# Eight feed-forward blocks, each with its own SBUF addresses for the split activations

## The reference

```python
def swiglu_ffn(h, w_in, w_out):            # h: [256, 1024], w_in: [1024, 5632], w_out: [2816, 1024]
    gate, up = jnp.split(h @ w_in, 2, axis=-1)
    return (jax.nn.silu(gate) * up) @ w_out

x = x + 0.5 * swiglu_ffn(rms_norm(x, gain), w_in, w_out)
```

## Time and profile before

| | value |
|---|---|
| median of two runs | 2578.5 us (2577.43 to 2579.57) |
| profiled execution, its own time | 2573.3 us |
| its span in the profile | 2571.5 us |
| TensorE busy, matmuls | 2499.3 us, 97% of the span, 23347 matmuls |
| VectorE busy | 1745.9 us, 68% |
| ScalarE busy | 1317.2 us, 51% |
| GpSimd busy | 79.1 us, 3% |
| read from HBM | 421.51 MB, 164 GB/s over the span |
| share of the chain that ended last: TensorE | 85% |

### The profile page before, as it was taken

The page is one execution under the profiler, slowest core; times in us unless marked ns, Lnnn a source line. Parts: engine busy times, 40 slices in busy tenths (PEclk is TensorE's granted clock), DMA queues, the critical chain, the costliest instruction groups (busy, mean ns, idle before and its releaser), DMA issues.

```text
span 2571.5 us, 60615 instructions
## 1 busy us (share of the span) xinstructions
PE 2499.3 (97%) x23347; PEld 2432.0 (95%) x23347; DVE 1745.9 (68%) x2868; ACT 1317.2 (51%) x1997; POOL 79.1 (3%) x122
## 2 busy tenths in 40 slices
PE   8998999999999999999999999899999999999999
PEld 8997877989999999989999999899999999999999
DVE  6757686667757667766756757967666566666774
ACT  5534544455545455555545547465455455555552
POOL 0000452000000000000000000000000000000000
PEclk9999999999999999999999999999999999999999
DMA  5663201535655664545654655245655565553564
GB/s 202 217 216 117 100 11 44 169 127 180 213 176 191 210 214 157 164 140 186 211 165 159 213 167 197 67 132 196 208 169 194 196 179 154 163 157 107 193 210 137
DMA packets 119825, 424.89 MB, mean 165 GB/s; under 512 B 16673, under 2 KB 24564, under 8 KB 119412
## 3 DMA queue, kind: packets, MB, share of 16 engines
q1 hardware_dynamic: 111616, 411.65, 48.4%
q10 hardware_dynamic: 8052, 11.04, 2.3%
HBM read 421.51 MB, written 1.12 MB: 164 GB/s over the span
## 4 chain that ended last, share of the span: by engine, by line
PE 85%; DVE 5%; ACT 2%; issue 2%; POOL 1%; DMA 0%; ACTq 0%; DVEq 0%; POOLq 0%
PE bank L478 19%; PE bank L472 19%; PE bank L477 19%; PE bank L398 5%; PE bank L400 4%; PE bank L399 4%; PE bank L2359 1%; ACT hi L341 1%; DVE lo L349 1%; PE bank L453 1%; PE bank L1761 1%; PE bank L454 1%; PE bank L455 1%; PE bank L1734 1%; PE bank L1280 1%
## 5 line engine op out<-in xcount | busy, mean ns | idle before, releaser
L349 DVE TENSOR_TENSOR lo<-raw,hi 128x1024 fp32r<-128x1024 f32 (+1 forms) x728 | 934.9, 1292 | 382.1 <-ACT hi L341 380.1
L341 ACT ACTIVATE hi<-raw 128x1024 fp32r<-128x1024 f32 (+1 forms) x728 | 782.7, 1106 | 302.8 <-PE bank L400 167.1
L472 PE MATMUL bank<-Hh,hi 128*128 128x256 f32 x3024 | 837.9, 277 | 3.3 <-DVE lo L349 2.0
L478 PE MATMUL bank<-Hh,lo 128*128 128x256 f32 x3024 | 838.5, 277 | 0.0
L477 PE MATMUL bank<-Hl,hi 128*128 128x256 f32 x3011 | 833.7, 277 | 0.0
L472 PEld LDWEIGHTS bank<-Hh,hi 128*128 128x128 f32 x3024 | 567.8, 188 | 4.5 <-DVE lo L349 4.3
L478 PEld LDWEIGHTS bank<-Hh,lo 128*128 128x128 f32 x3024 | 569.4, 188 | 0.0
L477 PEld LDWEIGHTS bank<-Hl,hi 128*128 128x128 f32 x3011 | 565.7, 188 | 0.0
L472 PE MATMUL bank<-Ah,hi 128*128 128x256 f32 x1408 | 389.8, 277 | 2.7 <-DVE lo L349 1.6
L478 PE MATMUL bank<-Ah,lo 128*128 128x256 f32 x1408 | 390.3, 277 | 0.0
L477 PE MATMUL bank<-Al,hi 128*128 128x256 f32 x1400 | 387.4, 277 | 0.0
(11 more groups left out here) (428 smaller groups left out, 4036.9 us busy)
## 6 DMA issues: line engine op xcount, KB each, us to landing
raw<-in_w SPq DMA_DIRECT2D x600, 512.0 KB, 3.4
raw<-in_w SPq DMA_DIRECT2D x128, 704.0 KB, 4.6
dB<-dil_bias ACTq DMA_DIRECT2D x16, 384.0 KB, 10.5
X<-in_x SPq DMA_DIRECT2D x2, 512.0 KB, 5.6
mem_x<-in_mem ACTq DMA_DIRECT2D x2, 512.0 KB, 3.3
gWS<-in_ws ACTq DMA_DIRECT2D x1, 1024.0 KB
gBS<-in_bs ACTq DMA_DIRECT2D x1, 1024.0 KB
out_x<-X SPq DMA_DIRECT2D x4, 256.0 KB, 2.6
```

The costliest lines, as they stand in the source:

```text
L341: act.activation(k.hi[:, q, :w], k.raw[:, q, :w], ACT.Copy).then_inc(k.hi_ready, 1)
L349: dve.tensor_tensor(k.lo[:, q, :w], k.raw[:, q, :w], k.hi[:, q, :w].bitcast(F32), ALU.subtract).then_inc(k.lo_ready, 1)
L472: pe.matmul(out, wh, xh, start=first, stop=False)
L478: mm = pe.matmul(out, wl, xh, start=False, stop=last)
```

## The change

The arena keeps `Hh`/`Hl` at 0 and 8 KB for the stages outside the feed-forward blocks. Each feed-forward block n gets tensors of its own: `Hh` at `PHASE_H[n][0]` and `Hl` at 8 KB + `PHASE_H[n][1]`; `Ah` at 40 KB + `PHASE_A[n][0]` and `Al` at 62 KB + `PHASE_A[n][1]`. All are multiples of 32 bytes, up to 192. To make room, `at` adds 128 bytes to every offset from 16 KB on and another 128 from 84 KB on, and the end of the arena moves up. The preparation of `Hh`/`Hl` in the block ahead writes to the home that belongs to the next block's gain. No instruction is added, removed or reordered, and no semaphore changes.

```diff
+PHASE_H = ((64, 128), (32, 32), (0, 64), (96, 160), (64, 160), (0, 32), (32, 96), (96, 128))
+PHASE_A = ((64, 96), (0, 96), (32, 128), (64, 64), (96, 192), (32, 64), (96, 96), (0, 0))
...
-        self.arena = sb("arena", [P, (self.room - 128) // 4])
-        self.limit = self.room - 128
+        self.arena = sb("arena", [P, (self.room - 64) // 4])
+        self.limit = self.room
...
-        self.Ah = self.at("Ah", self.A0, [P, FC, T], F32R)
-        self.Al = self.at("Al", self.A0 + 22 * KB, [P, FC, T], F32R)
+        self.H = {None: (self.Hh, self.Hl)}
+        self.A = []
+        for n, (h, a) in enumerate(zip(PHASE_H, PHASE_A)):
+            self.H[GAIN_OF[f"ffn{n}"]] = tuple(self.at(f"H{x}{n}", 8 * KB * j + h[j], [P, NC, T], F32R)
+                                               for j, x in enumerate("hl"))
+            self.A.append(tuple(self.at(f"A{x}{n}", self.A0 + 22 * KB * j + a[j], [P, FC, T], F32R)
+                                for j, x in enumerate("hl")))
...
     def at(self, name, offset, shape, dt=F32):
         size = 4 * int(np.prod(shape[1:]))
+        offset += P * ((offset >= 16 * KB) + (offset >= 84 * KB))
...
-    def pe_stage_h(self, pe, st, after_first=None, rest=False, pair=False, entry=False):
+    def pe_stage_h(self, pe, st, after_first=None, rest=False, pair=False, entry=False, gain=None):
         k, n = self.k, self.split_n["pe"] - NC
-        self.pe_stage(pe, st, lambda kg, kc: (k.Hh[:, kc, :], k.Hl[:, kc, :]),
+        Hh, Hl = k.H[gain]
+        self.pe_stage(pe, st, lambda kg, kc: (Hh[:, kc, :], Hl[:, kc, :]),
...
     def prep(self, eng, e, src, gain, c, split=True, square=True, wait=None):
         k = self.k
+        Hh, Hl = k.H.get(gain, k.H[None])
...
+        self.gain = GAIN_OF[name]
+        self.Ah, self.Al = self.k.A[order]
```

More of the change, by code:

```diff
@@ L529, in pe_stage, with pe_first_stage, pe_entry_stage @@
                 body(i)
-    def pe_first_stage(self, pe, st, pair=False):
+    def pe_first_stage(self, pe, st, pair=False, gain=None):
         self.split_n["pe"] += NC
-        self.pe_stage_h(pe, st, lambda: self.norm(pe, "pe"), pair=pair)
-    def pe_entry_stage(self, pe, st):
+        self.pe_stage_h(pe, st, lambda: self.norm(pe, "pe"), pair=pair, gain=gain)
+    def pe_entry_stage(self, pe, st, gain):
         k = self.k
         self.split_n["pe"] += NC
-        self.pe_stage_h(pe, st, entry=True)
-    def pe_stage_h(self, pe, st, after_first=None, rest=False, pair=False, entry=False):
+        self.pe_stage_h(pe, st, entry=True, gain=gain)
+    def pe_stage_h(self, pe, st, after_first=None, rest=False, pair=False, entry=False, gain=None):
         k, n = self.k, self.split_n["pe"] - NC
-        self.pe_stage(pe, st, lambda kg, kc: (k.Hh[:, kc, :], k.Hl[:, kc, :]),
+        Hh, Hl = k.H[gain]
+        self.pe_stage(pe, st, lambda kg, kc: (Hh[:, kc, :], Hl[:, kc, :]),
                       lambda kg, kc: pe.wait_ge(k.h_lo, n + kc + 1), after_first=after_first, rest=rest, pair=pair, entry=entry)
@@ L576, in prep @@
             if split:
-                eng.activation(k.Hh[:, c, :], src[:, c, :], ACT.Copy, scale=k.v1(gain, c)).then_inc(k.h_hi, 1)
+                eng.activation(Hh[:, c, :], src[:, c, :], ACT.Copy, scale=k.v1(gain, c)).then_inc(k.h_hi, 1)
             if square:
@@ L584, in prep @@
                 eng.wait_ge(k.h_hi, ns + 1)
-                eng.scalar_tensor_tensor(k.Hl[:, c, :], src[:, c, :], k.v1(gain, c),
-                                         k.Hh[:, c, :].bitcast(F32), ALU.mult, ALU.subtract).then_inc(k.h_lo, 1)
+                eng.scalar_tensor_tensor(Hl[:, c, :], src[:, c, :], k.v1(gain, c),
+                                         Hh[:, c, :].bitcast(F32), ALU.mult, ALU.subtract).then_inc(k.h_lo, 1)
             if square:
@@ L697, in pe @@
             sh.pe_keep_awake(pe, 5, k.X[:, 0, :P], k.X[:, 1, :])
-            sh.pe_entry_stage(pe, self.st_in)
+            sh.pe_entry_stage(pe, self.st_in, self.gain)
         else:
-            sh.pe_first_stage(pe, self.st_in)
+            sh.pe_first_stage(pe, self.st_in, gain=self.gain)
         done = 2 + FC * self.n
         sh.pe_stage(pe, self.st_out,
-                    lambda kg, kc: (k.Ah[:, kg * WIDE + kc, :], k.Al[:, kg * WIDE + kc, :]),
+                    lambda kg, kc: (self.Ah[:, kg * WIDE + kc, :], self.Al[:, kg * WIDE + kc, :]),
                     lambda kg, kc: pe.wait_ge(k.al_ready, done + WIDE * kg + kc + 1))
@@ L723, in body @@
                 act.wait_ge(k.a_ready, g + 3)
-                act.activation(k.Ah[:, bass.ds(m, 1), :].rearrange("p a t -> p (a t)"), k.act32[:, j, :],
+                act.activation(self.Ah[:, bass.ds(m, 1), :].rearrange("p a t -> p (a t)"), k.act32[:, j, :],
                                ACT.Copy).then_inc(k.ah_ready, 1)
@@ L761, in body @@
                 dve.wait_ge(k.a_ready, g + 3)
-                dve.tensor_tensor(k.Al[:, bass.ds(m, 1), :].rearrange("p a t -> p (a t)"), k.act32[:, j, :],
-                                  k.Ah[:, bass.ds(m, 1), :].rearrange("p a t -> p (a t)").bitcast(F32),
+                dve.tensor_tensor(self.Al[:, bass.ds(m, 1), :].rearrange("p a t -> p (a t)"), k.act32[:, j, :],
+                                  self.Ah[:, bass.ds(m, 1), :].rearrange("p a t -> p (a t)").bitcast(F32),
                                   ALU.subtract).then_inc(k.al_ready, 1)
```

## The result

The changed kernel takes 2624.09 us (2623.84 to 2624.33), the kernel before 2578.5 us. The ratio on record is 1.0189, with an interval of 1.0168 to 1.0211 (the two medians alone give 1.0177): the change costs time, and whether it costs a full 2% is not settled. The profiled execution has a span of 2622.5 us, 51.0 more than before. I had forecast no change, within 2548 to 2606 us; it came out 18 us above that range.

What follows compares the result with a forecast made beforehand. TensorE's start-to-start matmul time was taken as the bound; every part of the change was put at 0 us, so 2573.3 + 0 = 2573.3 us, as a median 2578.5 us, with a range of 2548 to 2606 us.

Steps and rivals of the forecast that it cites:

- What bounds the kernel: Dense stages: TensorE fills 97% of the span, and only the time from one matmul's start to the next matters.
- Writing the activations at other places: Ah copy and other split writes: 419 ns regardless of address, idle time covers any growth; 0 us, 7 us without cover.
- Reading the moving operand at another distance: 12672 feed-forward matmuls: distance from the weights has no part in the rhythm; 0 us, bounds +50 and -67 us.
- both cadences: Dense stages: quick, 113.1 ns a matmul, in fourteen feed-forward stages, and slow, 117.8 ns, in ffn6's two; preceding work decides.
- The shift of the rest of the arena: Mixers' and keys' tensors move 128 or 256 bytes against hi and lo; 0 us.
- The slower rival: Parted matmul, fourth slab: stops mending the cadence at new distances; 7.1 us a block, 2628 for seven; chance 0.17.
- The redraw: Each stage lands anew in one of two cadences; 2571 with ffn6 mended, 2593 with two blocks spoilt; chance 0.25.
- the quicker cadence: Dense matmuls: a distance avoids the two reads meeting, giving 111.6 or 108 ns; 2560 down to 2504 us; chance 0.16.

Runs made afterwards that it cites:

- e4: Changed kernel with Ah and Al offsets 0 and a different Hh/Hl offset pair, 0 to 128 bytes, in each block; ratio 1.0190.
- e6: Changed kernel with everything from 16 KB on shifted 256 bytes, Ah/Al offsets 0, new Hh/Hl pairs by block, 0 to 256 bytes; ratio 1.0063.
- e9: 256-byte shift from 16 KB on, Ah/Al offsets 0, only Hh or Hl off its good distance in each block; 2604.75 us, kernel before 2575.39.
- e1: Changed kernel with all sixteen offset pairs zero, leaving only the shift of 128 bytes from 16 KB and 256 from 84 KB; 2600.6 us, ratio 1.0092.

## Why the prediction was wrong

*What bounds the kernel*: right. TensorE's rhythm was the only quantity that mattered, and the feed-forward stages alone carried 46 of the 51 us.

*Writing the activations at other places, 0 us*: right; 419 ns before and after.

*Reading the moving operand at another distance, 0 us*: **this is the step that failed.** I argued that both cadences occur at one distance, so that addresses have no part. The rows showed only that distance is not the whole cause; at a single distance they could say nothing on what another would do. The bound that I had worked out, +50 us with all seven quick blocks slow, was nearly the answer: measured in its place were 46 us, 30 in the input stages and 16 in the output stages, with 117.3 to 119.2 ns a matmul where it had been 113.3. Two things act together: the distance decides which cadences a stage can keep, and the history (waits, the norm's matmul, the parted matmul) decides which of them it is in.

*The shift of the rest of the arena, 0 us*: wrong as well, and for the same reason. It moves `Ah` and `Al` by 128 bytes, and the shift alone cost 0.92%, 16 of 24 us in the output stages.

*The slower rival* (0.17) had the direction, nearly the price (7.1 us a block; measured are 46 us for seven blocks, 6.6 each) and nearly the end value (2628 against 2624.09, with 5 us from outside the blocks in it). Its mechanism was half right. The parted matmul does lead to the quick cadence at the old distance (and 256 bytes from it), and nowhere else. At 128 bytes off it did worse than fail: it ended the quick stretches. But it is not the whole of it: `Ah` and `Al` lost the quick cadence at the border of two stages with no parted matmul near, and input stages at the new distances were slow without any. I let the range end at four blocks of seven, as if blocks fell one by one. With the new offsets no feed-forward stage has both its halves at a multiple of 256 bytes from their old places (single halves have: `Hh` in ffn2 and ffn5, and after the shift `Al` in ffn2), so one cause moves all blocks together, and the rival should have stood in the range whole or been left out whole.

*The redraw* and *the quicker cadence*: in none of the profiles did a feed-forward stage settle below 113.3 ns. The redraw is real: with everything moved and no distance changed, ffn6's output stage turned quick (355 records from 2025 to 2065 us, against 342 in the earlier trace rows). At the offsets of the change it acts between slow values, as the run without parting shows.

The Trainium skill (SBUF — State Buffer, section "Who interferes with whom") says that TensorE never waits on anyone and has two independent read ports; by that rule the change is worth 0. Its first half is not touched by these runs, which compare TensorE with itself. Its second half does not hold here as a rule for time: the place of one of the two operands against the other, within 256 bytes, was worth 3 to 7 ns in every matmul. The formula of the Trainium skill (TensorE: Matmul & The Clock Gate, section "Back-to-back issue gap"), 109.2 ns for 256 columns, is given there for an isolated matmul and not for a stream with a weight load ahead of each; no feed-forward stage here came below 113.3 ns.

What stays open: why. A meeting of two streams of reads in some unit of the memory would repeat with a distance, but no run shows such a unit. Open as well is whether the quick cadence could last at 128 bytes off, since the six quick output stages seen there each met a parted matmul within 12.4 us.

## What to carry to other kernels

When a dense TensorE loop is the bound, count the starts in equal windows of each stage; a stage can lose 4% with no wait in the profile. Keep the streamed operand and the weights at the distance that measures best (here 192 bytes past a multiple of 256), and when a tensor of a dense stage must move, move it by 256 bytes. A value seen at one setting only is not evidence that the setting doesn't matter: carry its bound into the range whole.

## What the runs showed of the hardware

The start-to-start time of 128 x 256 fp32r matmuls, each with its own load of 128 weight columns, at the upper clock, settled at 113.3 ns at one of eight 32-byte positions and at 117 to 120 ns at the other seven, with a period of 256 bytes (scans e4, e6, e9). At the good position 117.8 ns is a second steady value. A wait of 0.18 us, or a float32 matmul in between, can lead into it, and a matmul split into 192 and 64 columns leads out of it most of the time. 128 bytes off, the same split matmul led from 113.3 to 117.8 ns, six times of six. A move of 128 bytes can undo a quick cadence from one matmul to the next, with no pause between them (e1).
